# Attention scores from two stacked products, a causal mask on the diagonal block, and a normalisation moved to ScalarE

## The reference

```python
# fox: c is a running sum of log gates, one number per head and token
s = q @ k.T / 8 + cq[:, None] - c[None, :]
s = where(kpos <= qpos, s, -1e30)
p = softmax(s);  out = p @ v
# dilated: three patterns (window, step) = (128,1) (512,4) (2048,16)
#   bias = -slope_h * (distance), each pattern a softmax of its own,
#   outputs mixed by the softmax denominators
```

## Time and profile before

| what | value |
|---|---|
| three executions | 2487.5, 2487.85, 2489.3 us |
| the profiled execution | 2487.53 us |
| its span in the profile | 2485.7 us |
| PE busy | 2457.6 us, 99% |
| DVE, ACT, POOL busy | 1797.5 (72%), 1167.2 (47%), 533.0 us (21%) |
| chain that ended last | PE 88%, DVE 8%, ACT 3% |
| first and last score product | 43.2 and 258.1 us |

### The profile page before, as it was taken

One profiled execution on the slowest core, in us unless ns is written; L12 is line 12 of the kernel. 1 busy time (PEld: TensorE's weight loads), 2 busy tenths in 40 slices (PEclk: granted clock), 3 DMA queues, 4 the chain that ended last, 5 costly groups with the idle time before them and its releaser, 6 DMA issues.

```text
span 2485.7 us, 35461 instructions
## 1 busy us (share of the span) xinstructions
PE 2457.6 (99%) x13593; PEld 2232.8 (90%) x13593; DVE 1797.5 (72%) x3334; ACT 1167.2 (47%) x1970; POOL 533.0 (21%) x342
## 2 busy tenths in 40 slices
PE   8999999999999999999999999999999999999998
PEld 7788888999999999999999999888888888888887
DVE  7876678998998886798898887877786335533323
ACT  6555466467767786333333334544422224422222
POOL 3222065132322342365554400000000000000000
PEclk9999999999999999999999999999999999999999
DMA  4211345588988998999999982222474323223331
GB/s 170 69 58 46 119 153 168 194 315 317 323 301 295 342 394 335 390 390 390 392 392 391 388 288 85 86 97 85 139 268 156 102 94 102 85 93 102 101 99 38
DMA packets 191239, 519.15 MB, mean 209 GB/s; under 512 B 15896, under 2 KB 67096, under 8 KB 187872
## 3 DMA queue, kind: packets, MB, share of 16 engines
q1 hardware_dynamic: 154208, 382.66, 43.8%
q0 software_dynamic: 36864, 134.23, 14.7%
HBM read 464.34 MB, written 52.49 MB: 208 GB/s over the span
## 4 chain that ended last, share of the span: by engine, by line
PE 88%; DVE 8%; ACT 3%; issue 1%; DMA 0%; DVEq 0%; SPq 0%; ACTq 0%
PE P L1295 27%; PE P L1297 27%; PE P L1296 27%; PE P L1642 2%; DVE wl L1754 1%; PE P L1302 1%; ACT wh L2405 1%; DVE T L1754 1%; DVE D L1754 1%; DVE RW L1754 0%; DVE RU L1754 0%; DVE T L1757 0%; PE P L1575 0%; PE P L1574 0%; PE P L1573 0%
## 5 line engine op out<-in xcount | busy, mean ns | idle before, releaser
L1295 PE MATMUL P<-XH,wh 128*128 128x512 f32 (+2 forms) x2272 | 845.1, 372 | 4.9 <-DVE QK L1757 2.5
L1297 PE MATMUL P<-XH,wl 128*128 128x512 f32 (+2 forms) x2272 | 823.1, 362 | 0.0
L1296 PE MATMUL P<-XL,wh 128*128 128x512 f32 (+2 forms) x2272 | 822.4, 362 | 0.0
L2405 ACT ACTIVATE wh<-raw 128x1024 fp32r<-128x1024 f32 x458 | 482.1, 1056 | 348.3 <-PE P L1297 340.2
L1754 DVE TENSOR_TENSOR wl<-raw,wh 128x1024 fp32r<-128x1024 f32 x420 | 509.2, 1220 | 75.0 <-ACT wh L2405 74.6
L1295 PEld LDWEIGHTS P<-XH,wh 128*128 128x128 f32 x2272 | 428.1, 188 | 50.0 <-issue 4.6
L1297 PEld LDWEIGHTS P<-XH,wl 128*128 128x128 f32 x2272 | 427.1, 188 | 47.6
L1296 PEld LDWEIGHTS P<-XL,wh 128*128 128x128 f32 x2272 | 428.0, 188 | 42.6 <-issue 1.9
L1295 PE MATMUL P<-AH,wh 128*128 128x384 f32 x1024 | 342.8, 335 | 1.3 <-DVE wl L1754 1.3
L1297 PE MATMUL P<-AH,wl 128*128 128x384 f32 x1024 | 342.1, 334 | 0.0
L1296 PE MATMUL P<-AL,wh 128*128 128x384 f32 x1024 | 342.1, 334 | 0.0
(11 more groups left out here) (329 smaller groups left out, 3269.2 us busy)
## 6 DMA issues: line engine op xcount, KB each, us to landing
raw<-wts SPq DMA_DIRECT2D x211, 512.0 KB, 3.6
raw<-ut SPq DMA_DIRECT2D x128, 512.0 KB, 6.5
raw<-vt SPq DMA_DIRECT2D x128, 512.0 KB, 12.0
hdram<-HID SPq DMA_DIRECT2D x64, 384.0 KB, 4.6
gdram<-GS SPq DMA_DIRECT2D x24, 1024.0 KB, 6.2
GI<-gdram SPq DMA_DIRECT2D x16, 1536.0 KB, 16.3
HI<-hdram SPq DMA_DIRECT2D x32, 768.0 KB, 16.7
AWC<-adat SPq DMA_DIRECT2D x64, 256.0 KB, 5.2
```

Of the source, the lines that this page charges most:

```text
L1295: e.matmul(bank, wh[:, w], H, start=start, stop=False)
L1296: e.matmul(bank, wh[:, w], L, start=False, stop=False)
L1297: return e.matmul(bank, wl[:, w], H, start=False, stop=stop)
L2405: return e.activation(dst, src, ACT.Copy)
```

## The change

Three edits, all in the attention.

1. Scores. Two products instead of three. q high stands over q low in one stationary tile (rows 0 to 63 and 64 to 127), and k high stands twice in one moving tile; their product is high by high plus low by high. The second product has q high with the position rows against k low with the position rows. The second copies of q high and k high are written by ACT at the end of `qk_split`, one copy of 64x1024 for q and one for k in each group (16 in all), and the scores wait for them (`s_qkd`).
2. Mask. For fox heads the mask matmul covers the diagonal 128 columns only. For dilated heads it stays whole.
3. Normalisation. For dilated heads DVE stops after the reciprocal and raises `s_rec`; ACT does the scaling in a new piece `normal` and raises `s_soft`. Fox heads stay on DVE.

POOL fills two tiles per set with zeros instead of four.

```diff
             def scores(n, g, h, qb):
+                p.wait_ge(s_qkd, 2 * g + 2)
                 e.matmul(bank[:, 0:kw], q[0][:, h, qs], q[2][:, h, 0:kw], start=True, stop=False)
-                e.matmul(bank[:, 0:kw], q[0][:, h, qs], q[3][:, h, 0:kw], start=False, stop=False)
-                e.matmul(bank[:, 0:kw], q[1][:, h, qs], q[2][:, h, 0:kw], start=False, stop=False)
-                mask = MDB if dilated(g) else MCB
-                e.matmul(bank[:, 0:kw], identb[:, :], mask[:, (3 - qb) * 128:T], start=False,
-                         stop=True).then_inc(s_scores, 1)
+                e.matmul(bank[:, 0:kw], q[1][:, h, qs], q[3][:, h, 0:kw], start=False, stop=False)
+                if dilated(g):
+                    e.matmul(bank[:, 0:kw], identb[:, :], MDB[:, (3 - qb) * 128:T], start=False,
+                             stop=True).then_inc(s_scores, 1)
+                else:
+                    e.matmul(bank[:, qs], identb[:, :], MCB[:, T - 128:T], start=False,
+                             stop=True).then_inc(s_scores, 1)
...
 # VectorE, qk_split
-                    H, L = q[2 * j][0:64, half, :], q[2 * j + 1][0:64, half, :]
+                    H = q[2 * j][0:64, half, :]
+                    L = q[0][64:128, half, :] if j == 0 else q[3][0:64, half, :]
...
 # VectorE, normal
+                if dilated(g):
+                    e.reciprocal(st[:, c + 3:c + 4], st[:, c + 2:c + 3]).then_inc(s_rec, 1)
...
 # ScalarE, end of qk_split
+                c.wait_ge(s_qkh, 4 * g + 2 * j + 2)
+                q = QK[g % 2]
+                H = q[2 * j][0:64, :, :].bitcast(F32)
+                copy(q[1][0:64, :, :] if j == 0 else q[2][64:128, :, :], H).then_inc(s_qkd, 1)
...
 # ScalarE
+            def normal(n, g, h, qb):
+                if dilated(g):
+                    c.wait_ge(s_rec, n + 1)
+                    p_ = TB[n % 5][:, 0:128 * (qb + 1)]
+                    c1 = 4 * (n % 4) + 3
+                    e.activation(p_, p_, ACT.Copy, scale=st[:, c1:c1 + 1]).then_inc(s_soft, 1)
```

More of the change, by code:

```diff
@@ L974, in build_program @@
         d_hi = [sem(f"d_hi{i}") for i in range(2)]
-        s_v, s_a, s_g = sem("s_v"), sem("s_a"), sem("s_g")
+        s_v, s_qkd, s_rec = sem("s_v"), sem("s_qkd"), sem("s_rec")
         s_high, s_low_v, s_low_p, s_used = sem("s_high"), sem("s_low_v"), sem("s_low_p"), sem("s_used")
@@ L1178, in positions @@
                 s.wait_ge(made[1], 16)
-                s.wait_ge(s_fill, 6 if g == 0 else 12)
+                s.wait_ge(s_fill, 4 if g == 0 else 8)
                 if g >= 2:
@@ L1184, in positions @@
                     s.wait_ge(d_posk, 16 * g)
-                e.dma_start(q[0][64:66, :, :].bitcast(F32), src[:, h0:h0 + 2, :]).then_inc(d_posq, 16)
-                e.dma_start(q[2][66:68, :, :].bitcast(F32), src[:, h0:h0 + 2, :]).then_inc(d_posk, 16)
+                e.dma_start(q[1][64:66, :, :].bitcast(F32), src[:, h0:h0 + 2, :]).then_inc(d_posq, 16)
+                e.dma_start(q[3][66:68, :, :].bitcast(F32), src[:, h0:h0 + 2, :]).then_inc(d_posk, 16)
             def forget(part):
@@ L1548, in scores @@
                 p.wait_ge(d_posk, 16 * (g + 1))
-                p.wait_ge(s_fill, 6 if g == 0 else 12)
+                p.wait_ge(s_fill, 4 if g == 0 else 8)
+                p.wait_ge(s_qkd, 2 * g + 2)
                 p.wait_ge(s_const, 3 if dilated(g) else 4)
                 e.matmul(bank[:, 0:kw], q[0][:, h, qs], q[2][:, h, 0:kw], start=True, stop=False)
-                e.matmul(bank[:, 0:kw], q[0][:, h, qs], q[3][:, h, 0:kw], start=False, stop=False)
-                e.matmul(bank[:, 0:kw], q[1][:, h, qs], q[2][:, h, 0:kw], start=False, stop=False)
-                mask = MDB if dilated(g) else MCB
-                e.matmul(bank[:, 0:kw], identb[:, :], mask[:, (3 - qb) * 128:T], start=False,
-                         stop=True).then_inc(s_scores, 1)
+                e.matmul(bank[:, 0:kw], q[1][:, h, qs], q[3][:, h, 0:kw], start=False, stop=False)
[5 more added lines that the diff above has]
+                             stop=True).then_inc(s_scores, 1)
             def turn(n, g, h, qb, t):
@@ L1906, in normal @@
                     own()
-                step(e.reciprocal(st[:, c + 3:c + 4], st[:, c + 2:c + 3]).then_inc(s_v, 1))
-                own()
-                e.tensor_scalar(p_[:, 0:kw], p_[:, 0:kw], st[:, c + 3:c + 4], None, ALU.mult).then_inc(s_soft, 1)
+                if dilated(g):
+                    e.reciprocal(st[:, c + 3:c + 4], st[:, c + 2:c + 3]).then_inc(s_rec, 1)
+                else:
+                    step(e.reciprocal(st[:, c + 3:c + 4], st[:, c + 2:c + 3]).then_inc(s_v, 1))
+                    own()
+                    e.tensor_scalar(p_[:, 0:kw], p_[:, 0:kw], st[:, c + 3:c + 4], None, ALU.mult).then_inc(s_soft, 1)
             def turn_low(n, g, h, qb, t):
@@ L2504, in qk_split @@
                 for half in range(2):
-                    H, src = QK[g % 2][2 * j][0:64, half, :], bank[64 * half:64 * half + 64, :]
+                    q, src = QK[g % 2], bank[64 * half:64 * half + 64, :]
                     if j == 0:
-                        e.activation(H, src, ACT.Copy, scale=-0.125).then_inc(s_qkh, 1)
+                        e.activation(q[0][0:64, half, :], src, ACT.Copy, scale=-0.125).then_inc(s_qkh, 1)
                     else:
-                        copy(H, src).then_inc(s_qkh, 1)
+                        copy(q[2][0:64, half, :], src).then_inc(s_qkh, 1)
+                c.wait_ge(s_qkh, 4 * g + 2 * j + 2)
+                q = QK[g % 2]
+                H = q[2 * j][0:64, :, :].bitcast(F32)
+                copy(q[1][0:64, :, :] if j == 0 else q[2][64:128, :, :], H).then_inc(s_qkd, 1)
             def v_copy(g):
@@ L2762, in _ @@
             work = {f.__name__: f for f in (
-                high, gained, near, counts, square, root, gain, table, norm, forget, qk_split, v_copy, v_turn, soft, turn, values, subkeys, query, key,
+                high, gained, near, counts, square, root, gain, table, norm, forget, qk_split, v_copy, v_turn, soft, normal, turn, values, subkeys, query, key,
                 token, gate, gate_turn, weigh, grid, hidden, rows, dots_end, mod_load, mod_part, rotation, square2,
@@ L2794, in fill @@
                 for j in range(2):
-                    for i in range(4):
+                    for i in (1, 3):
                         if n:
@@ L2799, in fill @@
                         n += 1
-                    for i, value in ((0, -1.0), (2, 1.0)):
+                    for i, value in ((1, -1.0), (3, 1.0)):
                         g.wait_ge(s_fill, n)
```

## The result

| | median us | lowest to highest | runs | span of the profiled execution |
|---|---|---|---|---|
| before | 2487.99 | 2487.49 to 2490.00 | 18 | 2485.7 |
| changed | 2493.09 | 2492.76 to 2493.50 | 18 | 2491.0 |

The ratio is 1.0019, 95% interval [1.0012, 1.0026]. The forecast was 2480.6 with a range up to 2486.5: wrong in sign. The gain in PE's queue is there, but ScalarE, which got two new jobs, takes it back and more.

What follows compares the result with a forecast made beforehand. PE was taken as the bound in the attention. Start +2.55, new waits +3.65, old waits gone -2.0, dilated products -4.6 and fox -6.8 made -7.2 us: median 2480.6, 8 in 10 range 2475 to 2486.5.

Steps and rivals of the forecast that it cites:

- The queue: PE's queue in the attention: 12.2 us shorter, 10.8 from 64 matmuls removed and 1.4 from the fox masks cut.
- the 0.8 of the first steps: Saving of the five products before the transpose of step 1, 0.8 us, taken as lost in PE's wait there.
- The start: First dilated steps: duplicate and moved scaling in ACT's queue make PE 2.55 us late at the transpose of step 1.
- The walk: Instruction-by-instruction bookkeeping of the first steps: transpose of step 1 starts at 63.3 instead of 60.77.
- the wait for PTL that was to go: Dilated half: an old PE wait of 0.8 us behind PTL, part of 2.0 us of old waits expected to vanish.
- from step 16 to 19 the scalings are 0.6 us or more ahead of the transposes, and I take it so to the end: Later dilated steps: no new PE waits for ACT's scaling after step 15; new waits total 3.65 us.
- the terms +2.55, +3.65, -2.0 and -4.6: Dilated half, in us: late start, new PE waits for scalings, old waits gone, products saved in steps 5 to 31.
- the fox duplicates at nothing: Fox half: 8 duplicates on ACT cost nothing, hidden by cover; without cover at most 1.05 us each.
- (a): Rival, chance 0.21: all of PE's saving arrives, -11.4 to -13.4 us, 2475.3 at the middle.
- (b): Rival, chance 0.22: dilated half saves nothing and the start costs 1.85 us of extra clock; -2.4 us, 2485.4.
- (c): Rival, chance 0.06: DVE and ACT alternation becomes the bound, 3.9 us a dilated step; +7.8 us, 2495.6.
- (d): Rival, chance 0.03: stationary loads set the pace, so PE's queue is not shortened; +2.55 us or more, 2490.

Runs made afterwards that it cites:

- products and mask alone: Changed kernel with the dilated scaling back on VectorE and without the 16 duplicates, so cross terms of the scores are missing: 2478.22 us.
- The kernel with the filled wait: Changed kernel with 18 unused 128x128 matmuls put into PE's 4.2 us wait before the transpose of step 1: 2492.81 us.
- the scaling and no duplicates: Changed kernel without the 16 second copies of q high and k high, whose rows stay zero: 2491.82 us, ratio 1.0014.
- The hand-over: Two-product scores and short mask, no duplicates, VectorE scaling; added: ScalarE waits for each dilated reciprocal, then copies one unused column: 2482.91 us.
- the time: Two-product scores and short mask, no duplicates, VectorE scaling; added: scaling-shaped ScalarE copies on an unused buffer, steps 3 to 31, no wait: 2480.44 us.

## Why the prediction was wrong

**The queue: right, the products a little large.** The mask gave 1.0 to 1.4 us against 1.4. The products gave 8.3 to 8.8 instead of 10.0 (10.8 less the 0.8 of the first steps). By the table, products and mask alone have -0.28 us at step 11 and -3.16 at step 31, not -4.6: the saving is lost not in 5 steps but in about the first 12. The fox half gave 6.2 us against 6.8; why 0.6 is missing stays open.

**The start: right.** The walk gave 63.3 for the transpose of step 1; it starts at 63.43. ACT's queue, against the earlier trace rows:

```profile
50.62 1.06 ACT L2412 ACTIVATE QK<-QK 64x1024 fp32r<-64x1024 f32 x1
...
53.94 0.73 ACT L2545 ACTIVATE T<-P,st 128x128 f32<-128x128 f32 x2
55.47 0.40 ACT L2555 ACTIVATE T<-T,st 128x128 f32<-128x128 f32 x1 [0.80 <-DVE st L1912]
...
62.41 0.58 ACT L2545 ACTIVATE T<-P,st 128x384 f32<-128x384 f32 x1
```

The duplicate takes 1.06 us (1.05 forecast), the exponentials start at 53.94 and 62.41 (53.95 and 62.45). The bookkeeping holds beyond the start too: by the same terms PE is some +3.7 us late at step 15 and +0.9 at step 23 (2.55 + 3.65 - 2.0 - 3.3 for the products of steps 5 to 23), and it is +3.82 and +2.06. It gets there partly another way: from 64 to 97 us PE waits 0.5 us and not 3.65, since part of that time it runs at the half clock (granted 0.83 in 60 to 80 us). The kernel with the filled wait, which has no such spell there, is as late from step 9 on. Of the 1.1 us at step 23, most is the wait for PTL that was to go and stayed, 1.02 us at 109.55. The scalings are dearer than the 0.6 taken at width 512 (groups of ACT, 43 to 270 us: busy us, mean ns, idle before):

```profile
L2555 ACT ACTIVATE T<-T,st 128x512 f32<-128x512 f32 x8 | 5.8, 723 | 3.5 <-DVE st L1912 3.4
...
L2555 ACT ACTIVATE T<-T,st 128x128 f32<-128x128 f32 x8 | 3.2, 403 | 2.8 <-DVE st L1912 2.8
```

**The step that failed most: "from step 16 to 19 the scalings are 0.6 us or more ahead of the transposes, and I take it so to the end".** The prediction saw the loop (ACT waits for DVE's reciprocal, DVE's next piece for ACT's copy PTH), priced it at 3.2 us against a pace of 3.30, and let the waits end after step 15. From mask 11 to mask 23 that held: the changed kernel takes 3.32 us a step, as products and mask alone do (3.33), and before took 3.47. In the last dilated group, steps 24 to 31, it takes 3.82 where before took 3.34. There the forecast gains 1.35 us and the kernel loses 3.8, nearly all of it in the two waits of 1.78 and 2.88 us for the scaling. This is one turn of the loop in the changed kernel, all rows in their order (PE's matmuls and DVE's short reads of the sum left out):

```profile
83.46 0.16 DVE L1912 RECIPROCAL st<-st 128x1 f32<-128x1 f32 x1
83.66 0.72 ACT L2555 ACTIVATE T<-T,st 128x512 f32<-128x512 f32 x1 [0.44 <-DVE st L1912]
84.28 0.47 ACT L2412 ACTIVATE PTH<-P 128x384 fp32r<-128x384 f32 x1
...
84.79 0.56 DVE L1757 TENSOR_TENSOR PTL<-P,PTH 128x384 fp32r<-128x384 f32 x1 [1.17 <-ACT PTH L2412]
85.26 0.41 DVE L1898 TENSOR_REDUCE st<-P 128x1 f32<-128x256 f32 x1
85.59 0.28 DVE L1907 CUSTOM_DVE_ANT_0 T<-T,CNT 128x128 f32<-128x128 f32 x1
85.71 0.47 ACT L2545 ACTIVATE T<-P,st 128x256 f32<-128x256 f32 x1 [0.96 <-DVE st L1898]
...
85.92 0.16 DVE L1912 RECIPROCAL st<-st 128x1 f32<-128x1 f32 x1
```

Reciprocal to reciprocal is 2.46 us here, well inside the pace. What the sum of the loop left out, and the walk took in only up to step 19, is the side work that stands in ACT's queue inside some turns: a copy of a weight unit (1.05 us), the splits (1.2 each pair), the duplicate, MH, v. While ACT does it, DVE's next piece waits, where before it had more to do meanwhile. DVE's waits for PTH in 80 to 150 us rose, before and after:

```profile
DVE PTL L1754 <- ACT PTH L2405: 3.0, 5, 1.0
```

```profile
DVE PTL L1757 <- ACT PTH L2412: 13.4, 13, 1.5
```

The start of the exponentials gives the mean pace from step 5 to step 32: 3.36 us a step before (68.05 to 158.76), 3.24 with products and mask alone, 3.53 in the changed kernel, 3.64 with the scaling and no duplicates. The worst turn, in the last dilated group, shows the side work in one row behind the other, on ACT, ahead of the scaling for which PE waits 2.88 us:

```profile
147.46 1.19 ACT L2412 ACTIVATE QK<-P 64x512 fp32r<-64x512 f32 x2
148.69 1.06 ACT L2412 ACTIVATE QK<-QK 64x1024 fp32r<-64x1024 f32 x1
149.77 1.06 ACT L2412 ACTIVATE wh<-raw 128x1024 fp32r<-128x1024 f32 x1
...
152.86 0.37 ACT L2545 ACTIVATE T<-P,st 128x128 f32<-128x128 f32 x1 [1.00 <-DVE st L1898]
154.06 0.72 ACT L2555 ACTIVATE T<-T,st 128x512 f32<-128x512 f32 x1 [0.83 <-DVE st L1912]
```

One group earlier the same three rows ran from 116.12 to 119.50, the exponential and the scaling followed without a wait, and no wait of PE of 0.2 us or more came of it. Here MH and PTH stand in between, and then the exponential waits 1.00 us and the scaling 0.83 us for DVE. That the side work is the cause is read from these rows; no run moves it by itself. It is not a plain sum either: the duplicates are side work too, and without them the dilated half is later (+8.07), not earlier.

So PE is at +5.88 us at the end of the dilated half, not at the -0.4 that the terms +2.55, +3.65, -2.0 and -4.6 make. That is 6.3 of the 12.5 us between forecast and result, 5.2 of them in steps 24 to 31.

**The second step that failed: the fox duplicates at nothing.** The prediction showed a cover of 1.8 us at one step of width 512. The step that matters is another, of width 384, where DVE's scaling runs beside POOL's subtraction. Before:

```profile
194.15 2.39 POOL L2788 TENSOR_TENSOR wl<-raw,wh 128x1024 fp32r<-128x1024 f32 x1 [10.21 <-ACT wh L2405]
...
195.09 1.67 DVE L1909 TENSOR_SCALAR T<-T,st 128x384 f32<-128x384 f32 x1
...
197.03 0.49 PE L1302 MATMUL P<-ident,T 128*128 128x128 f32 x3
```

It ended at 196.76, 0.27 us ahead of its transpose: the cover was not 1.8 but 0.27 us. After:

```profile
199.87 1.06 ACT L2412 ACTIVATE QK<-QK 64x1024 fp32r<-64x1024 f32 x1
200.83 1.04 ACT L2412 ACTIVATE wh<-raw 128x1024 fp32r<-128x1024 f32 x1
...
201.94 2.60 DVE L1916 TENSOR_SCALAR T<-T,st 128x384 f32<-128x384 f32 x1
201.95 2.38 POOL L2806 TENSOR_TENSOR wl<-raw,wh 128x1024 fp32r<-128x1024 f32 x1 [9.63 <-ACT wh L2412]
```

The duplicate delays the weight copy, that delays POOL's subtraction, and this now meets DVE's scaling over its whole length: 2.60 us for 128x384, ending at 204.54, where the earlier trace rows has 0.49 for 128x512. The transpose at 204.60 is late by 0.96. The rule weighed in the prediction (the Trainium skill, SBUF — State Buffer, Who interferes with whom) names this operation too, a tensor_scalar in a two-port mode; the prediction applied it only to the product with the counts. The trace agrees: DVE is held, 2.60 us for 128x384 against 0.42 in the step of 168.28 before, while POOL takes its usual 2.38. Which of the two came first, 0.01 us apart, the trace can't tell. With VectorE scaling it shows in the dilated half as well (896 against 421 ns above), where the duplicates make PE 4.2 us later at step 31 (+1.01 less -3.16). In the table the fox half shows three parts that add up: -6.20 for products and mask, +3.13 for duplicates (-3.07 less -6.20), +2.21 for what the late dilated steps and their scalings spill into it (-3.99 less -6.20); together -0.86, and measured is -0.74. That is 6.1 us short of the forecast -6.8, the other half of the error. The third part shows as PE's waits for PTL at 169 and 175 us; the prediction had nothing for it.

**The rivals.** (a) is false. (b) had a second dip of the clock, and it came, 0.83 in 60 to 80 us, but the filled wait shows that it cost nothing in the end. Its mark was seen and its price was wrong. (c), at 0.06, named a loop that is slower than PE, with the decision at 3.62 us a step. Over the whole dilated half the changed kernel takes (157.19 - 43.85) / 31 = 3.66 by the masks, start included, but the loop is slower than PE in the last group (3.82) and not from mask 11 to mask 23 (3.32). The time, 2493.1, came out nearest to (c)'s 2495.6, and that is luck: (c) has PE 14.6 us late at step 31 and a whole fox gain of 6.8, against +5.88 and 0.74. Its causes were half right: the scalings do take 0.72 us at 512, but the products with the counts did not get slower (735 ns at 512, against 952 in the earlier trace rows). (d) is false: products and mask alone gave 9.8 us.

**What stays open.** Why the changed kernel is less late at step 31 (+5.88) than the one without its duplicates (+8.07). The traces point to the phase against POOL's subtraction, though no run tests it: with the duplicates the products with the counts meet it less. With them, and without them (DVE, 43 to 160 us):

```profile
L1907 DVE CUSTOM_DVE_ANT_0 T<-T,CNT 128x384 f32<-128x384 f32 x7 | 4.9, 705 | 0.0
```

```profile
L1906 DVE CUSTOM_DVE_ANT_0 T<-T,CNT 128x384 f32<-128x384 f32 x7 | 7.6, 1083 | 0.0
```

## What to carry to other kernels

When an operation moves to an engine that must wait for the one it came from, follow the whole of that engine's queue to the end of the stage, not the operations of the loop alone and not its first steps: from then on the two take turns, and side work in the wrong place holds up both. The hand-over (4.7 us) and the time (2.2) cost 11.1 us together, so they have to be priced together. A cover read at one step is not the cover: look for the step with the least, where another engine's long instruction lies beside the chain. A copy that no engine has to make, as a duplicate of rows, can go to a DMA queue with room.

## What was not expected of the hardware

A copy of 64x1024 takes ACT 1.06 us, as long as one of 128x1024 (1.05): half the partitions save nothing, as the prediction took it. An in-place multiplication by a scale per row takes ACT 0.40, 0.51, 0.62 and 0.72 us at 128 to 512 columns, where DVE needs 0.29 to 0.49 when nothing disturbs it; a plain in-place copy of 128x512 takes 0.62 to 0.63.

The granted clock does not follow the length of a wait alone. The kernel with the scaling back on VectorE had waits of 2.64 and 3.09 us and a granted clock of 1.00 in both stretches to 80 us; the changed one fell to 0.90 and 0.83 after waits of 2.63 and 4.18. The Trainium skill (TensorE: Matmul & The Clock Gate, Part 1) has an idle array fall back to the half clock. These runs show the fall, and also waits of like length without it; what decides it they do not show.
